# A tuned hybrid encoder layer: one VectorE addition moved up, the load queue of the down stage reordered, and the last tile's scaling split over two engines

## What is computed

```
def conv_ffn(h, w_up, w_conv, b_conv, w_down):
    u = causal_dwconv(h @ w_up, w_conv, b_conv)
    gate, up = jnp.split(u, 2, axis=-1)
    return (jax.nn.silu(gate) * up) @ w_down
...
    x = x + conv_ffn(rmsnorm(x, norm2_g), w_up, w_ffn_conv, b_ffn_conv, w_down)
return rmsnorm(x, final_g)      # y * rsqrt(mean(y*y) + eps) * g
```

## Time and profile before

| | us |
|---|---|
| median of 3 runs | 1054.2 (1054.15 to 1054.25) |
| the profiled execution's own time | 1054.37 |
| its span from first to last instruction | 1052.6 |
| PE busy | 1024.2 (97%) |
| DVE busy | 728.0 (69%) |
| ACT busy | 500.2 (48%) |
| POOL busy | 74.4 (7%) |

### The profile page before, as it was taken

One profiled execution on the slowest core, in us unless ns is written; L12 is line 12 of the kernel. 1 busy time (PEld: TensorE's weight loads), 2 busy tenths in 40 slices (PEclk: granted clock), 3 DMA queues, 4 the chain that ended last, 5 costly groups with the idle time before them and its releaser, 6 DMA issues.

```text
span 1052.6 us, 13256 instructions
## 1 busy us (share of the span) xinstructions
PE 1024.2 (97%) x4933; PEld 845.9 (80%) x4933; DVE 728.0 (69%) x1153; ACT 500.2 (48%) x939; POOL 74.4 (7%) x80
## 2 busy tenths in 40 slices
PE   5999999999989999799999999999999999999997
PEld 4888888888778888688888888888888887888886
DVE  5352555641675567898778777777787778996796
ACT  7632445443653324465445445454454634444564
POOL 5020222220330000000000000000000000000000
PEclk9999999999999999899999999999999999999999
DMA  7126111110242224233223122231230998125104
GB/s 223 43 73 149 40 31 30 40 41 21 62 140 81 80 80 140 60 101 115 66 81 100 60 94 88 80 100 60 81 101 21 362 391 306 59 86 186 58 1 161
DMA packets 108640, 107.75 MB, mean 102 GB/s; under 512 B 13330, under 2 KB 81032, under 8 KB 108576
## 3 DMA queue, kind: packets, MB, share of 16 engines
q1 hardware_dynamic: 107040, 103.56, 31.1%
q0 software_dynamic: 1536, 3.34, 1.3%
HBM read 86.93 MB, written 19.96 MB: 102 GB/s over the span
## 4 chain that ended last, share of the span: by engine, by line
PE 91%; DVE 4%; ACT 2%; DMA 2%; issue 1%; SPq 0%; DVEq 0%; POOL 0%; ACTq 0%; POOLq 0%
PE pz L1815 19%; PE pz L2112 7%; PE pz L2113 7%; PE pz L2114 7%; PE pd L2112 6%; PE pd L2114 6%; PE pd L2113 6%; PE pd L2136 4%; PE pd L2133 4%; PE pd L2135 4%; PE pd L2043 3%; PE pd L2041 3%; PE pd L2042 3%; PE pz L2133 3%; PE pz L2136 3%; PE pz L2135 3%
## 5 line engine op out<-in xcount | busy, mean ns | idle before, releaser
L1016 ACT ACTIVATE ws_hi<-raw 128x512 fp32r<-128x512 f32 x88 | 52.9, 626 | 107.8 <-PE pz L2114 52.1
L1815 PE MATMUL pz<-h_hi,w_hi 128*128 128x512 f32 x304 | 99.2, 399 | 2.6 <-DVE h_lo L1203 2.6
L2112 PE MATMUL pz<-ht_hi,ws_hi 128*128 128x512 f32 x240 | 94.7, 395 | 5.3 <-DVE u L1597 5.3
L1815 PE MATMUL pz<-h_lo,w_hi 128*128 128x512 f32 x304 | 96.8, 391 | 0.0
L1815 PE MATMUL pz<-h_hi,w_lo 128*128 128x512 f32 x304 | 96.3, 390 | 0.0
L2113 PE MATMUL pz<-ht_lo,ws_hi 128*128 128x512 f32 x240 | 94.5, 394 | 0.0
L2114 PE MATMUL pz<-ht_hi,ws_lo 128*128 128x512 f32 x240 | 94.3, 393 | 0.0
L2112 PE MATMUL pd<-ht_hi,ws_hi 128*128 128x512 f32 x200 | 77.8, 389 | 0.0
L2113 PE MATMUL pd<-ht_lo,ws_hi 128*128 128x512 f32 x200 | 77.8, 389 | 0.0
L2114 PE MATMUL pd<-ht_hi,ws_lo 128*128 128x512 f32 x200 | 77.8, 389 | 0.0
L1620 DVE SCALAR_TENSOR_TENSOR gate<-u,vec,gate 128x1023 f32<-128x1023 f32 (+1 forms) x44 | 56.5, 1284 | 20.0 <-ACT gate L1058 19.2
(11 more groups left out here) (297 smaller groups left out, 2495.7 us busy)
## 6 DMA issues: line engine op xcount, KB each, us to landing
raw<-in_w_up SPq DMA_DIRECT2D x48, 512.0 KB, 4.8
b<-in_w_down SPq DMA_DIRECT2D x49, 256.0 KB, 7.2
act_rows<-gate SPq DMA_DIRECT2D x22, 512.0 KB, 2.7
a<-act_rows SPq DMA_DIRECT2D x44, 256.0 KB, 5.4
raw<-in_w_in SPq DMA_DIRECT2D x14, 512.0 KB, 3.7
x_in<-in_x SPq DMA_DIRECT2D x8, 512.0 KB, 6.0
x_again<-in_x SPq DMA_DIRECT2D x8, 512.0 KB, 4.1
b_raw<-in_w_down SPq DMA_DIRECT2D x14, 256.0 KB, 6.3
```

The costliest lines, as they stand in the source:

```text
L1016: nc.scalar.activation(ws_hi[m][:, :, :], summand(p, i), ACT.Copy).then_inc(s["ws_hi_made"], 1)
L1815: ins = mm(dst[:, h * HALF:(h + 1) * HALF], w[:, c], v[:, h * HALF:(h + 1) * HALF], start=first, stop=last)
L2112: mm(dst, wh[:, k, :], xh[:, k, :], start=begins and k == 0, stop=False, skip_group_check=not begins)
```

## The change

Three edits, and a fourth that makes room for them. `add_11(0)` is moved from the end of DVE's preparation of the first pair to the place behind its second weight split. In the down stage's load queue the streamed tiles come first, then `a21`, and the `x_whole` tiles stand one by one behind k = 4, 6 and 8; `y_add` moves two steps back (to steps 7 to 10 of a phase). At the end the first half of tile 3 is multiplied by the gain early on DVE and by its root factor late on ACT, while DVE does the second half; the eight small `ms` activations are made together ahead of the last squares. Two semaphores of the start (gain_turned, gain_ready) are merged into vec_turned and vec_ready, which count one more.

```diff
@@ SP
             for k in range(STREAM_RING):
                 load_stream(k)
-            for k in range(3):
-                load_a21(k)
             for i in range(NT // 2):
                 sp.wait_ge(x1_stored[i], 64)
...
-            for (m, half), block_ in x_whole.items():
+
+            def load_x1(m, half):
                 rows = x1_d[m * HALF:(m + 1) * HALF, half * HALF:(half + 1) * HALF]
-                sp.dma_start(block_[:, :, :], rows.rearrange("(t p) c -> p t c", p=P)).then_inc(s["x1_loaded"], 16)
+                sp.dma_start(x_whole[m, half][:, :, :], rows.rearrange("(t p) c -> p t c", p=P))\
+                  .then_inc(s["x1_loaded"], 16)
+
             for k in range(STREAM_RING, KT):
                 load_stream(k)
+                load_a21(k - STREAM_RING)
+                if k in (4, 6, 8):
+                    load_x1(*((0, 0), (1, 0), (1, 1))[k // 2 - 2])
+            for k in range(KT - STREAM_RING, KT):
                 load_a21(k)
...
-                    sp.wait_ge(s["y_made"], 2 * n + half + 1)
+                    if n == NT - 1 and half == 0:
+                        sp.wait_ge(s["y_half_made"], 1)
+                    else:
+                        sp.wait_ge(s["y_made"], 2 * n + half + (n < NT - 1))
@@ ACT
+            def y_mean(i):
+                half = i // 4
+                act.wait_ge(s["x2_squared"], (4 if half else 0) + i % 4 + 1)
+                nc.scalar.activation(ms3[:, i:i + 1], ss3[:, i, half:half + 1], ACT.Identity, bias=eps[:, :],
+                                     scale=1.0 / D).then_inc(s["x2_mean"], 1)
...
+            for i in range(NT):
+                y_mean(i)
             for i in range(4, NT):
                 y_square(i, 0)
                 y_root(i - 4, i)
             for i in range(4):
                 y_square(i, 1)
                 y_root(4 + i, i)
+            act.wait_ge(s["x2_rstd"], NT)
+            act.wait_ge(s["y_gained"], 1)
+            nc.scalar.activation(x_block[0, 0][3], x_block[0, 0][3], ACT.Copy, scale=rstd[:, 3:4])\
+                .then_inc(s["y_half_made"], 1)
@@ DVE
             sum_low(0, 6)
             sum_low(0, 7)
+            add_11(0)
             sum_add(0, 3)
...
             for i in range(FT):
-                add_11(i)
+                if i:
+                    add_11(i)
...
-                for half in range(2):
+                for half in range(n == NT - 1, 2):
...
-                ph, t = n // KT - 1, n % KT - 5
+                ph, t = n // KT - 1, n % KT - 7
...
             dve.wait_ge(s["final_g_loaded"], 32)
+            dve.wait_ge(s["x2_squared"], 4)
+            nc.vector.tensor_tensor(x_block[0, 0][3], x_block[0, 0][3], final_gb[0][:, :], ALU.mult)\
+                .then_inc(s["y_gained"], 1)
```

More of the change, by code:

```diff
@@ L330, in hymba_kernel @@
         bank = [pz[0][:, 0:HALF], pz[0][:, HALF:], pz[1][:, 0:HALF], pz[1][:, HALF:]] + [p[:, :] for p in pd]
-        names = """table_loaded gain_loaded gain_turned gain_ready vec_loaded vec_turned vec_ready
+        names = """table_loaded gain_loaded vec_loaded vec_turned vec_ready
             small_loaded gate_w_loaded const_made mem_made
@@ L351, in hymba_kernel @@
             down_summed down_hi_made down_split down_used down_done y_added x1_loaded final_g_loaded
-            x2_squared x2_mean x2_rooted x2_rstd y_made y_stored""".split()
+            x2_squared x2_mean x2_rooted y_gained y_half_made x2_rstd y_made y_stored""".split()
         s = {n: sem(n) for n in names}
@@ L743, in h_high @@
                 if n == 0:
-                    act.wait_ge(s["gain_ready"], 1)
+                    act.wait_ge(s["vec_ready"], 1)
                 act.wait_ge(s["x_turned"], n + 1)
@@ L773, in z_keep @@
                 j = b - 1
-                act.wait_ge(s["vec_ready"], 1)
+                act.wait_ge(s["vec_ready"], 2)
                 if j == MO:
@@ L1102, in y_square @@
                                      accum_out=ss3[:, i, half:half + 1]).then_inc(s["x2_squared"], 1)
-            def y_root(n, i):
[L1105 to L1110, removed]
+            def y_mean(i):
[3 more added lines that the diff above has]
+                                     scale=1.0 / D).then_inc(s["x2_mean"], 1)
+            def y_root(n, i):
+                half = 1 - i // 4
+                act.wait_ge(s["x2_squared"], (12 if half else 8) + i % 4 + 1)
+                act.wait_ge(s["x2_mean"], NT)
+                nc.scalar.activation(root[:, i:i + 1], ss3[:, i, half:half + 1], ACT.Sqrt, bias=ms3[:, i:i + 1],
+                                     scale=1.0 / D).then_inc(s["x2_rooted"], 1)
             wa_high(2, 2)
@@ L1180, in after @@
                 dve.wait_ge(s["dve_step"], steps[0])
-            dve.wait_ge(s["gain_turned"], 1)
-            nc.vector.tensor_copy(vec[:, 0:NK], bank[7][:, 0:NK]).then_inc(s["gain_ready"], 1)
+            dve.wait_ge(s["vec_turned"], 1)
+            nc.vector.tensor_copy(vec[:, 0:NK], bank[7][:, 0:NK]).then_inc(s["vec_ready"], 1)
             def spread_gates():
@@ L1217, in vectors @@
             def vectors():
-                dve.wait_ge(s["vec_turned"], 3)
+                dve.wait_ge(s["vec_turned"], 4)
                 nc.vector.tensor_copy(vec[:, NK:VEC_A], bank[4][:, NK:VEC_A])
@@ L1783, in _ @@
             pe.wait_ge(s["gain_loaded"], 16)
-            nc.tensor.transpose(bank[7][:, 0:NK], vec_rows[0:NK, 0, :], ident[0:NK, 0:NK]).then_inc(s["gain_turned"], 1)
+            nc.tensor.transpose(bank[7][:, 0:NK], vec_rows[0:NK, 0, :], ident[0:NK, 0:NK]).then_inc(s["vec_turned"], 1)
             def turn_x(i, features):
@@ L1789, in turn_x @@
                     if i == 0 and k == NK - 1:
-                        pe.wait_ge(s["gain_ready"], 1)
+                        pe.wait_ge(s["vec_ready"], 1)
                     if i == NT // 2 and k >= 6:
```

## The result

The changed kernel takes 1055.8 us (median of 22 runs, 1053.4 to 1058.1), the kernel before, run beside it, 1053.5 (22 runs, 1052.0 to 1054.4). The ratio is 1.0022 with a 95% interval from 1.0016 to 1.0029: 2.4 us slower, just past the 2.1 us that I had called the limit of what can be told. The profiled execution of the changed kernel took 1054.64 (span 1052.9), near the low end of its own runs, while that of the kernel before, 1054.37, was at the high end of its own. Compared alone, the two profiles show 0.3 us, and the medians about nine times that.

The account below looks back on a forecast made before the run. PE, with 91% of the chain, was taken as the bound, through its waits, slow clock and tail. -2.0 + 2.3 - 0.3 = 0.0 on the profiled 1054.37, carried to the median: 1054.2 us, range 1050.2 to 1056.0.

Parts of the forecast that it names:

- Part 1: Up stage, first pair: moving the addition cuts PE's 5.3 us wait to about 3.3 before product 4; net -2.0 us.
- -5.0: Up stage: how many us earlier the stage would be if PE came back at full clock.
- +3.0: Up stage: us lost to a clock fall behind the new 3.3 us wait, priced from the old fall there.
- three times within 0.1 us: Up stage: earlier times' closeness, taken as evidence against the same wait's clock price varying between executions (-5.0 to -2.0).
- Part 2: Down stage: new load queue removes the 1.3 us wait, but the late third x tile delays step 19; net +2.3 us.
- 23.0 in all: Down-stage load queue: us for 17 units between streamed tile 3 and the third x tile's landing, at 387 GB/s.
- my list of issues keeps it full: Down-stage load queue: argument that the queue would not run dry again, though each streamed load waits for a split.
- Rival (d): Down stage: third x tile later still, queue at 344 GB/s, 17 units taking 25.9 us; 1057.1 us, chance 0.12.
- Rival (c): Down stage: x tiles not late, overtaking streamed ones or the queue draining faster; 1049.2 us, chance 0.10.
- Part 3: Kernel's end: ACT and DVE scale both halves side by side, so the second store issues earlier; -0.3 us.

Follow-up runs that it names:

- e_part1: The kernel before with only add_11(0) moved up: 1050.77 us against 1052.96, ratio 0.9977.
- e_part2: The kernel before with only the new load queue and the later y_add: 1057.63 us against 1052.96, ratio 1.0045.
- e_part2_xwait: e_part2 with product 1's y_add waiting only for the first x tile, product 6's for the other two: 1055.59 us against 1053.50 for the kernel before.
- e_queue_fixed: Kernel before with first x tile ahead of streamed tile 3, other two last, y_add later and awaiting its own tile: 1050.45 us against 1052.96.
- e_part3: The kernel before with only the split tail and the merged semaphores: 1052.90 us against 1052.96, ratio 1.0000.
- e_part2_x_first: e_part2 with the first x tile issued ahead of streamed tile 3: 1053.52 us against 1053.50 for the kernel before, ratio 0.9996.
- e_part1_both: The kernel before with add_11(0), keep_22(0) and add_22(0) all moved up: 1046.51 us against 1052.96, ratio 0.9934.
- e_best: e_part1_both with the split tail added: 1046.49 us against 1052.96 for the kernel before, ratio 0.9933.
- e_best_queue: e_best with the rebuilt load queue of e_queue_fixed: 1044.09 us against 1052.96 for the kernel before, ratio 0.9913.

## Why the prediction was wrong

I forecast no change. The measured 1055.8 lies in the range that I gave (1050.2 to 1056.0), but by luck: the range was laid around a level that was 0.7 us too high (see the end of this section). Around the level of 22 runs it would have ended at 1055.3. Part for part (from the ratios): -2.4, +4.7 and 0.0 make +2.3, and the ratio of the whole is worth +2.3 as well, so the parts add up; I had -2.0, +2.3 and -0.3.

**Part 1 held.** The new wait at product 4, its cause, its time (440.1 against 440.04) and the net -2.0 (-2.4) all came as worked out. Part of that is luck. The -5.0 counts a fall of 3.0 that goes, and the +3.0 a fall that comes, so the -2.0 is the shorter wait alone and needs only that both falls cost the same. The 3.0 itself was read from one execution, the dearest of eight with this wait; the other seven paid 1.4 to 1.8. Behind the new wait it was 1.6 in one profiled execution (the changed kernel) and 3.0 in another (e_part1). That three times within 0.1 us speak against a varying price did not hold. Over 22 executions the kernel before spreads over 2.4 us. The Trainium skill ("TensorE: Matmul & The Clock Gate", section "What's actually happening") had it right, that the moment of the transition varies from run to run; the two executions of one kernel above agree, 1.7 us apart at one wait.

**Part 2 is the step that failed, by its size.** The mechanism came as described: idle DMA engines, the x tile late, DVE held at `y_add`, PE at step 19 (3.7 us, forecast 3.1), the clock down behind it. In the profile the stage lost 3.6 (forecast 2.3), in e_part2's 4.05, and in the median of e_part2 4.7. One term was mis-sized, and one delay was overlooked:

1. "23.0 in all", 17 units at 387 GB/s. They took 25.35 us (weight half of tile 3 landed at 855.85 + 3.2 = 859.05, the third x tile at 873.89 + 10.5 = 884.4), 352 GB/s in the mean. I wrote that "my list of issues keeps it full"; but after an idle stretch each streamed load still waits for a split, and so up to 864 the queue was not full. That tile 3 landed faster on an empty queue (3.2 us, not 5.1) gave 1.8 us back, of which I had counted 0.7. In the time of the old trace (3.29 later) `y_add` stood until 887.72 and not 886.4, which is 2.35 - 1.8 + 0.7 = 1.3 later, and step 22 started 1.3 later too (900.2 and not 898.9): the whole miss in the profile. Rival (d) named this mechanism. Rival (c) leaned on a wrong reading, that everything in the old queue landed 9 to 11 us behind its issue: the earlier trace rows has a load that took 5.1.
2. A second late tile that I didn't look for: the streamed tile of step 20 stands in the queue behind the third x tile. e_part2_xwait shows it as 2.1 us once the first cause is gone. It doesn't add to the 3.7 us wait, but it means that the wait had no slack behind it. The wait at step 18 (0.4 us in the changed kernel, 0.8 in e_part2) is of the same kind, since its tile stands behind the second x tile. With only the first x tile ahead of the streamed ones, in the idle stretch (e_queue_fixed), no wait is left.

What the median of e_part2 adds to its profile's 4.05 lies within the interval. The mean granted clock (0.9932 against 0.9949) says that part of the median's loss is clock; the fall in the profile is that of one execution. I can't divide it further.

**Part 3** happened as described and bought nothing that can be measured. The term had the last store's issue as the end and left out the transfers behind it, which by the DMA rows of e_part3 set the end; no run takes them away, so that is read from the rows and not tested.

**The level.** I took the median of three runs, 1054.2, for the kernel's time. Twenty-two give 1053.5. This made the forecast time wrong by 0.7 us in the other direction.

## What to carry to other kernels

When a wait is taken away, list what is queued behind it on every engine until nothing waits; moving one instruction gained 2.4 us, moving it together with the two it uncovered 6.9. In a load queue, put each load where its first user needs it, and let each user wait for its own tile alone: a large tile that nobody needs yet delays both its own waiter, if that counts all tiles, and whatever is queued behind it. And don't count on the full rate right behind an idle stretch when each load is released by a buffer: here the queue gave 240 and 285 GB/s for eight us before it was back at 380.

## What was not expected of the hardware

What a wait costs in clock differed from execution to execution. Behind the same 5.3 us wait the fall cost 3.0 us in one profiled execution and 1.4 to 1.8 in seven; behind the same 3.3 us, 1.6 in the changed kernel and 3.0 in e_part1; behind the same 1.8 us wait, in two executions of one kernel, 0 and 1.7. Behind 2.1 us in the dense part of the down stage neither of two executions showed a fall, while e_part2_x_first had one there behind 2.0 us (granted clock 0.78 from 884 to 888 and 0.79 from 888 to 892).

So a single profile is one sample, and it can lie some us from the median: e_part2_xwait was profiled at 1052.87, its median is 1055.59. The times spread over 2.4 us before and 4.7 after (22 executions each). Whether a kernel without the long waits spreads less is not shown: five executions each of e_part1_both, e_best and e_best_queue spread over 1.2, 2.1 and 1.2 us, but five of e_part2, which has all the waits, spread over 2.1 too.
